# First attention of a two-block kernel: the scores as three products of split q and k

## The reference

```python
q = rope(rmsnorm(q, q_norm_gain[i]), cos, sin)
k = rope(rmsnorm(k, k_norm_gain[i]), cos, sin)
...
s = jnp.einsum('bqhcd,bkhcd->bhcqk', qblk, k).astype(jnp.float32) * scale
qpos = bi * Q_BLOCK + jnp.arange(Q_BLOCK)
mask = kpos[None, :] <= qpos[:, None]
s = jnp.where(mask, s, neg)
p = jax.nn.softmax(s, axis=-1)
a = p[:, :, 0] - lam * p[:, :, 1]
return jnp.einsum('bhqk,bkhe->bqhe', a.astype(v.dtype), v)
```

## Time and profile before

| | us |
|---|---|
| median of 3 runs (1495.84 to 1496.68) | 1496.06 |
| the profiled execution's own time | 1496.67 |
| its span, first to last instruction | 1494.9 |
| TensorE busy, of the span | 1422.2 (95%) |
| ScalarE busy | 826.3 (55%) |
| VectorE busy | 638.2 (43%) |

### The profile page before, as it was taken

One profiled execution on the slowest core, in us unless ns is written; L12 is line 12 of the kernel. 1 busy time (PEld: TensorE's weight loads), 2 busy tenths in 40 slices (PEclk: granted clock), 3 DMA queues, 4 the chain that ended last, 5 costly groups with the idle time before them and its releaser, 6 DMA issues.

```text
span 1494.9 us, 18265 instructions
## 1 busy us (share of the span) xinstructions
PE 1422.2 (95%) x6750; PEld 1111.7 (74%) x6750; DVE 638.2 (43%) x1126; ACT 826.3 (55%) x1153; POOL 203.5 (14%) x235
## 2 busy tenths in 40 slices
PE   3999999999899999999999999899989999999994
PEld 2887777677578788888888877677758888888883
DVE  4884345565533435555145154656242201212124
ACT  4644666676564565666355376554566545535331
POOL 0120110010011111111111111110101111111111
PEclk9999999999999999999999999999999999999997
DMA  7889866556369878888878895654647888888861
GB/s 253 196 172 184 204 158 148 134 121 147 85 147 235 182 180 187 191 194 195 206 174 195 211 223 145 151 131 113 142 112 168 199 193 186 199 188 183 198 147 56
DMA packets 80675, 255.34 MB, mean 171 GB/s; under 512 B 16592, under 2 KB 17744, under 8 KB 80464
## 3 DMA queue, kind: packets, MB, share of 16 engines
q0 software_dynamic: 32544, 118.50, 44.0%
q1 hardware_dynamic: 47616, 132.57, 29.1%
q10 hardware_dynamic: 432, 3.15, 0.6%
HBM read 128.09 MB, written 3.41 MB: 88 GB/s over the span
## 4 chain that ended last, share of the span: by engine, by line
PE 86%; DVE 5%; ACT 4%; DMA 2%; issue 1%; SPq 1%; POOLq 0%; POOL 0%; DVEq 0%; ACTq 0%
PE pg L491 26%; PE pg L493 26%; PE pg L492 26%; PE ps L637 2%; PE py L701 1%; DMA toep<-k_dram 1%; DVE x_lo L1288 1%; PE ps L770 1%; PE px L654 1%; PE ps L780 1%; DMA w_lo<-w_raw 1%; DVE hid L1288 1%; DMA w_raw<-weights 1%; PE py L790 1%; ACT w_lo L872 0%
## 5 line engine op out<-in xcount | busy, mean ns | idle before, releaser
L491 PE MATMUL pg<-x_hi,w_hi 128*128 128x512 f32 x1184 | 476.7, 403 | 12.8 <-DVE x_lo L1288 12.0
L492 PE MATMUL pg<-x_lo,w_hi 128*128 128x512 f32 x1184 | 464.5, 392 | 0.0
L493 PE MATMUL pg<-x_hi,w_lo 128*128 128x512 f32 x1184 | 464.1, 392 | 0.0
L459 POOL DMA_DIRECT2D w_lo<-w_raw x226 | 194.8, 862 | 1250.8 <-ACT w_lo L872 1224.3
L871 ACT ACTIVATE w_hi<-w_raw 128x1024 fp32r<-128x1024 f32 x226 | 237.5, 1051 | 128.7 <-PE pg L493 112.6
L491 PEld LDWEIGHTS pg<-x_hi,w_hi 128*128 128x128 f32 x1184 | 223.9, 189 | 72.3 <-issue 13.4
L492 PEld LDWEIGHTS pg<-x_lo,w_hi 128*128 128x128 f32 x1184 | 224.4, 189 | 48.3 <-issue 3.7
L493 PEld LDWEIGHTS pg<-x_hi,w_lo 128*128 128x128 f32 x1184 | 224.0, 189 | 47.4
L872 ACT ACTIVATE w_lo<-w_raw 128x1024 fp32r<-128x1024 f32 x226 | 236.4, 1046 | 0.0
L493 PE MATMUL pg<-act_hi,w_lo 128*128 128x512 f32 x432 | 170.4, 394 | 0.0
L491 PE MATMUL pg<-act_hi,w_hi 128*128 128x512 f32 x432 | 170.4, 394 | 0.0
(11 more groups left out here) (257 smaller groups left out, 1453.3 us busy)
## 6 DMA issues: line engine op xcount, KB each, us to landing
w_raw<-weights SPq DMA_DIRECT2D x226, 512.0 KB, 4.6
w_lo<-w_raw POOLq DMA_DIRECT2D x226, 512.0 KB, 5.5
kq_rot<-kq_raw SPq DMA_DIRECT2D x64, 64.0 KB, 2.4
hid<-x SPq DMA_DIRECT2D x4, 512.0 KB, 5.6
hid<-x ACTq DMA_DIRECT2D x1, 2048.0 KB, 11.2
out<-hid SPq DMA_DIRECT2D x8, 256.0 KB, 2.0
u_dram<-hid SPq DMA_DIRECT2D x4, 256.0 KB, 6.9
pairs<-u_dram SPq DMA_DIRECT2D x8, 128.0 KB, 6.9
```

Source lines behind the costliest of these rows:

```text
L459: pool.dma_start(w_lo[:, s], w_raw[:, s], accum_op=ALU.add).then_inc(lo_in[s], 16)
L491: pe.matmul(bank[:], wh, xh(k), start=n == 0, stop=False)
L492: pe.matmul(bank[:], wh, xl(k), start=False, stop=False)
L493: last = pe.matmul(bank[:], wl, xh(k), start=False, stop=n == len(ks) - 1)
```

## The change

For each head, q and k after rope are no longer written to `qq` and `kk` in float32. VectorE's last rope operation writes into `kq_rot` and signals `turned_raw`. ScalarE rounds that into `qq_hi` or `kk_hi` (float32r) and signals `turned_hi`; VectorE subtracts the rounded from the raw into `qq_lo` or `kk_lo` and signals `roped`. `scores` does three float32r products in place of one in float32: high by high, q high by k low, q low by k high, each for both 64-row halves in turn. The low parts take the memory of `y5`, which is free by then.

```diff
@@ scores
-                for c in range(2):
-                    r = slice(64 * c, 64 * c + 64)
-                    pe.matmul(bank[:, c, 0:w], qq[r, h % 2, P * i:P * i + P], kk[r, h % 2, 0:w], start=True, stop=False)
+                for q_half, k_half in ((qq_hi, kk_hi), (qq_hi, kk_lo), (qq_lo, kk_hi)):
+                    for c in range(2):
+                        r = slice(64 * c, 64 * c + 64)
+                        pe.matmul(bank[:, c, 0:w], q_half[r, h % 2, P * i:P * i + P], k_half[r, h % 2, 0:w],
+                                  start=k_half is kk_hi and q_half is qq_hi, stop=False)
@@ ScalarE
+            def turned_high(h, n, dst):
+
+                act.wait_ge(turned_raw, 2 * h + n + 1)
+                if h >= 2:
+                    act.wait_ge(maxed, EXPS[("s", h - 2, QB - 1)] + 1)
+                act.activation(dst[:, h % 2], kq_rot[:, n], ACT.Copy).then_inc(turned_hi, 1)
+
...
                 if h < HEADS:
                     ahead(("k", h))
+                if attends:
+                    turned_high(g, 1, qq_hi)
+                if h < HEADS:
                     kq_out(h, "k", 0, "kg")
...
                     exps1(g, 3)
                 if h < HEADS:
+                    turned_high(h, 0, kk_hi)
                     ahead(("v", h))
@@ VectorE
-                put(tt_(dst[:, h % 2], rope_a[:], kq_rs[:, n]), roped)
+                put(tt_(kq_rot[:, n], rope_a[:], kq_rs[:, n]), turned_raw)
+
+            def turned_low(h, n, dst, high):
+
+                dve.wait_ge(turned_hi, 2 * h + n + 1)
+                put(tt_(dst[:, h % 2], kq_rot[:, n], high[:, h % 2].bitcast(F32), ALU.subtract), roped)
...
+                if attends:
+                    turned_low(g, 1, qq_lo, qq_hi)
                 if h >= 2:
                     turned(h - 2, 3)
...
                 if h < HEADS:
-                    rope_step(h, "q", 1, rs_q, qq)
+                    turned_low(h, 0, kk_lo, kk_hi)
+                    rope_step(h, "q", 1, rs_q)
```

More of the change, by code:

```diff
@@ L208, in build @@
             gates = sb("gates", [P, 16, T], scope=first)
-            y5 = sb("y5", [P, SSM_T, T], scope=first)
+            with ExitStack() as s:
+                y5 = sb("y5", [P, SSM_T, T], scope=s)
+            kk_lo = sb("kk_lo", [P, 2, T], F32R, scope=first)
+            qq_lo = sb("qq_lo", [P, 2, T], F32R, scope=first)
             with ExitStack() as s:
@@ L223, in build @@
                 kq_rot = sb("kq_rot", [P, 2, T], scope=s)
-                kk = sb("kk", [P, 2, T], scope=s)
-                qq = sb("qq", [P, 2, T], scope=s)
+                kk_hi = sb("kk_hi", [P, 2, T], F32R, scope=s)
+                qq_hi = sb("qq_hi", [P, 2, T], F32R, scope=s)
                 v_raw = sb("v_raw", [P, T], scope=s)
@@ L330, in build @@
         act_c, dve_c = sem("act_c"), sem("dve_c")
+        turned_raw, turned_hi = sem("turned_raw"), sem("turned_hi")
         roped, maxed, combed, o_sq, o_done = (sem(n) for n in ("roped", "maxed", "combed", "o_sq", "o_done"))
@@ L1057, in _ @@
                 ahead(("ssm", n))
+                if n == 1:
+                    turned_high(0, 0, kk_hi)
             ahead(("v", 0))
@@ L1573, in turned, with rope_step @@
                 ps_read(dve, ("t", h, i))
-            def rope_step(h, name, n, ready, dst):
+            def rope_step(h, name, n, ready):
                 evacuated(dve, (name, h))
@@ L1590, in _ @@
             link(ts(rtab[64:96, 1], rtab[64:96, 1], -1.0, ALU.mult))
-            rope_step(0, "k", 0, rs_k, kk)
+            rope_step(0, "k", 0, rs_k)
             for n in range(4):
                 ssm_out(n)
-            rope_step(0, "q", 1, rs_q, qq)
+            turned_low(0, 0, kk_lo, kk_hi)
+            rope_step(0, "q", 1, rs_q)
             for h in range(1, HEADS + 2):
@@ L1614, in _ @@
                 if h < HEADS:
-                    rope_step(h, "k", 0, rs_k, kk)
+                    rope_step(h, "k", 0, rs_k)
                 if attends:
```

## The result

The changed kernel takes 1505.88 us in the median (1504.79 to 1506.62), the kernel before 1495.95 in the same runs: 9.9 us more, a ratio of 1.0064 with an interval of 1.0048 to 1.008. The forecast was 1502.0 us with a range of 1499 to 1508. The direction and the range held; 5.9 us more were forecast, and 9.9 were measured.

What follows compares the result with a forecast made beforehand. TensorE bounds the kernel, held at first scores by ScalarE's pt copy. Blocks +0.2, head 0 -0.3, heads 2 to 6 +4.3, head 7 +1.7: +5.9 us, 1502.0 us; own range 1500 to 1505, whole range 1499 to 1508.

Steps and rivals of the forecast that it cites:

- What bounds the kernel: Whole kernel: TensorE, busy 95%; at the first scores of heads 1 to 6 it waits 0.44 us for ScalarE's pt copy.
- The score blocks: Scores: three float32r products, halves side by side; blocks 0 and 1 +0.03 us a head, 2 and 3 -0.30.
- dearer blocks: Rival at the scores: halves in turn, loads exposed or narrow products at float32's rate; 1504.5 to 1509.5 us; chance 0.19.
- The splits of k and q: ScalarE and VectorE before the first scores: copies and subtractions delay the pt copy, +0.86 us at heads 2 to 6.
- the sign to look for: Ahead of the first block of heads 2 to 6: a wait of 1.3 us in place of 0.44.
- the 0.30 of blocks 2 and 3: Scores, two widest blocks: 1.61 us in place of 1.91, a saving that ends in the wait except at head 0.
- 8 x 0.03: Scores of all heads: blocks 0 and 1 take 1.09 us in place of 1.06, +0.2 us in the sum.
- Head 7: First scores of head 7, no tile ahead: chain +2.2 us, less about half a us for the clock; +1.7 taken.
- 5 x 0.86 = +4.3: First scores of heads 2 to 6: the longer wait for the pt copy, +4.3 us in the sum.
- Hidden splits: Rival at the first scores: ScalarE's copy of q is done before the k tile ends; 1497.6 us; chance 0.11.
- faster: Rival at the scores: products cost only their streams and splits are hidden under the tiles; 1487 us; chance 0.05.
- 8 x 0.70 and 8 x 0.28: Dearer prices of blocks 0 and 1 over eight heads: halves in turn 0.70 us, loads exposed by the skill's rule 0.28.

Runs made afterwards that it cites:

- e4: Kernel before (float32 scores, no splits) with the pt copy moved ahead of kq_out, the k tile's evacuation, on ScalarE: 1493.07 us, ratio 0.9977.
- e2: Changed kernel with all its copies, subtractions and waits, but scores does one float32 product of the high parts: 1502.74 us, ratio 1.0045.
- e6: Kernel before with needless ScalarE copies of 512 columns, 1024 columns or both ahead of kq_out: ratios 1.0021, 1.005 and 1.0103.
- e1: Changed kernel without splits: q and k written once in float32r, scores multiplies the same pair three times: 1494.7 us, ratio 0.9993.
- e10: Changed kernel with k's subtraction behind q's rope, pt copy ahead of kq_out, and head 7 kept in float32: 1492.82 us, ratio 0.9982.
- dummy1: Kernel before with one needless ScalarE copy of 512 columns ahead of kq_out: ratio 1.0021.

## Why the prediction was right, and where it fell short

*What bounds the kernel.* Right: TensorE, and ahead of the first scores ScalarE's queue. e4 shows it by removal.

*The score blocks.* Predicted 0.54, 0.55, 0.72, 0.89 us; measured 0.48, 0.55, 0.72, 0.91 in the trace after. The halves run side by side, and the loads of the second and third product stay hidden. The rival "dearer blocks" falls. The rule of the Trainium skill, "TensorE: Matmul & The Clock Gate", Part 3, that a load overlaps matmuls only where the row group differs, made 0.59 us of block 0 by the prediction's estimate. The measured 0.48 is not enough against it, since 0.1 of the 0.59 was the change back to whole-array matmuls. The distances decide. With its load of 107 ns exposed, a product would start 0.16 us behind the one before it at 128 columns, and 0.32 at 512, as an estimate; the third products start 0.11 and 0.24 behind the second, and the loads stand beside the matmuls of the same half. The trace does not agree with the rule here.

*The splits of k and q.* Predicted: 0.86 us at heads 2 to 6 by the queue, nothing at heads 0 and 1. Measured in e2, where the blocks are as before: the wait rises from 0.44 to 1.28, 0.84. Head 1 keeps its 0.44 in the changed kernel. In the changed kernel the wait is 1.57, not the 1.3 that I named as the sign to look for: I had said that the 0.30 of blocks 2 and 3 ends in the wait, and then did not add it to the wait. For the sum it is neutral, and the period of 28.0 us came out as said. Blocks 0 and 1 together take 1.03 us where 1.09 was forecast, so that 8 x 0.03 is not there either.

*Head 7.* +2.2 us for the chain was right (2.19). For the clock behind it I took 0.5 us off, and the stretch grew from 6.8 to 10.2 us instead, which costs 0.4: 2.6 in place of 1.7, inside the bounds of 1.2 to 4.7.

*The step that was mis-sized* is that the clock was considered at head 7 alone. In the sum "5 x 0.86 = +4.3" each wait has the price of its length; two of the five also brought a slow stretch worth 1.7 us, 3.3 us together. That is most of the 3.9 between forecast and result; 0.9 more are head 7's, and the blocks give some 0.4 back. The trace of before could not give the number, since its waits were either 0.44 us alone or, ahead of head 7, 3.3 of 5 us idle in all, but the earlier trace rows showed that idle time has a second price, and the term belonged into the range of heads 2 to 6 as well. Only e6 gave the length from which it counts here.

*The range.* The forecast's own range of 1500 to 1505 us missed 1505.88. The wide range of 1499 to 1508 held only because it had been drawn for dearer blocks, which did not come: that part is luck.

*The rivals.* "Hidden splits" falls by e2, "faster" by e1, which gets 2.4 us in its stage at best. Two prices of the dearer blocks, 8 x 0.70 and 8 x 0.28, are counted against the kernel before and were put on top of a forecast that already held 8 x 0.03: each is 0.2 us too high, which changes nothing.

## What to carry to other kernels

Work that looks free on an engine at 55% has a place in that engine's order; ask what stands behind it there and which buffer that frees. When one engine's part gets shorter ahead of a gate that another engine sets, the wait grows by as much, and a longer wait can cost more than itself: here a kernel with slower products (e2) was no slower, and by its median faster, than the one with faster products. Before speeding up products, look at the order of the jobs on the engine that TensorE waits for: exchanging two lines (e4) brought 3 us, more than the products could.

## What the runs showed of the hardware

- Ahead of the first scores of heads 1 to 6, a wait of TensorE of up to 1.28 us once in some 27 us was followed by no fall of the granted clock in any of the nine profiles with such waits; waits of 1.39, 1.57 and 1.91 us were followed by a stretch of 3.4 us at 1.2 GHz in some heads and not in others (3 of 6, 5 of 15 over three profiles, 4 of 6). Each stretch cost about 1.7 us. What decides between heads with the same wait was not tried. At head 7 two more waits, of 0.7 to 1.2 us, stand a few us ahead of the last one, and the clock fell in all fourteen profiles: for 10.2 us in the six where the last wait was 2.5 us or more, for 6.8 us in six and 3.4 us in two (e10, dummy1) of the eight where it was 1.0 to 1.7 us.
- float32r products of 64 rows and 128 columns, with a weight load each, started 0.16 us (first to second) and 0.11 us (second to third) apart in a row half while the other half did the same; the block of 128 columns took 0.48 us.
- A copy of 128x512 from float32 to float32r took 0.43 us on VectorE and 0.63 on ScalarE.
